# Sample attention of a hybrid decoder step: value gathers asked for after the logits, and all key turns between logits and products

## The chip, the core and the metric

The kernel runs on one core of one Trainium2 chip. The metric is the device time of one launch in microseconds (us). The kernel before takes 1688.96 us, the median of three runs (1687.34 to 1699.0).

## What is computed

The reference is one layer of a decoder, for a prompt group (512 tokens) and a sample group (8 sequences of 8 new tokens, 64 rows in all). What matters here is the attention of the sample group. For each of its 64 rows an indexer has picked 256 keys out of 4096 cached ones; their keys and values are gathered from a paged cache, and every row attends to its own 256 keys (and to new ones where they were picked):

```
def attend_selected(q, kg, vg, valid):
    logits = jnp.einsum('bqhd,bqkhd->bqhk', q, kg).astype(jnp.float32) * (HEAD_DIM ** -0.5)
    logits = jnp.where(valid[:, :, None, :], logits, -jnp.inf)
    p = jax.nn.softmax(logits, axis=-1).astype(vg.dtype)
    return jnp.einsum('bqhk,bqkhd->bqhd', p, vg)
```

There are 8 heads of 64 columns, so a gathered row of keys or of values is 512 float32, 2 KB.

## The kernel before, in words

Every engine runs one long list of jobs, in an order that a planner writes down before the program is built (`JOBS`). TensorE (PE), ScalarE (ACT) and VectorE (DVE) walk lists made from the same plan, so the plan sets what waits behind what on each of them. GpSimd (POOL) has its own list in the code, and issues the gathers.

**The sample attention** works on 16 groups (`NGR`) of 4 rows (`GQ`). For group g:

- `gather_keys(g, j)` (L873, POOL): two indirect DMAs of 128 rows of 2 KB for row j into `kunit`. For g > 0 it first waits until the same place was turned for the group before.
- `T(g, j)` (`turn_keys`, L991, PE; `keys_act`, L1378, ACT): 8 transposes of row j's keys into two PSUM banks, and two copies into `kts`. ACT first waits for the logits of the group before, which read `kts`. PE's next turn waits for the copy before the last.
- `QK(g)` (`logits`, L1002 and L1008, PE): 4 matmuls with the bias (8 records) and 16 with the keys (32 records), each 8 output rows wide in its own quarter of the array. It waits for `OM` of the group before and for the last copy of the keys. At its end it raises `lg_full`.
- `max` (L1848 and L1849, DVE), then `EX` (L1384, ACT): the row maximum and the exponentials. `PT` (L1017 and L1018, PE; L1392, ACT): three transposes of the weights and a copy.
- `gather_values(g)` (L883, POOL): eight indirect DMAs into `vunit`; they wait for `pv_done` of the group before, which read `vunit`.
- `PV(g)` (`values`, L1026 and L1029, PE): the products with the values; it waits for each row's values. Then `om` (L1860, DVE), and `OS(g)` (`own_rows`, L1036, PE).

POOL's order is: the keys of group 0; then for each g the keys of rows 0 to 2 of g + 1, the values of g, and the keys of row 3 of g + 1.

**The plan** around it (`interleaved`): `prompt_jobs` is the prompt's work. It begins with gate projections (`gcP`, `gcS`, L962). Then come its *units*: index scores `pi` (24 jobs, L1087 on PE, L1757 on DVE), 32 attention units `qk`, `pt`, `pv` (L1096, L1103, L1109), with the convolution's norm (`cv`, `croot`, `cn`) and its projection (`cbP`, `cbS`, L1135) between them. Last come the projections `gaP`, `gaS` and `abP`. `sample_jobs` lists the pieces of the sample attention. `cost` gives each job a price on PE in us: a `T` 0.9, `QK` 3.4, `PT` 0.5, `PV` 2.7, `OS` 0.9, `gaP` and `gcP` 6.9, `gaS` and `gcS` 1.8, `abP` and `cbP` 3.5, an index score 0.22 for each 128 keys and so on. `vector_cost` does the same for DVE. The planner puts prompt jobs, and whenever DVE's running total is more than 6 ahead of PE's, it puts pieces of the sample attention until it is not. After the units the pieces left are spread evenly over the jobs left.

In the plan before, QK(0) ends at 24.4 of planned PE time, QK(9) at 164.9; the units end at 249.4 (with group 9's products asked for among them, and no piece in the last 72.8), and the whole list at 411.0.

**DVE's list** (`vector_jobs`) follows the same order, with work of its own in it: 62 taps of the depthwise convolution (L1740 and L1742), all of them ahead of the first index score; and after the scores of each of three prompt tiles 16 rounds of the top-128 selection (L1766 and L1767), of which one is put behind each of DVE's jobs until they run out. The rounds of a tile must be done before that tile's first attention unit.

PE and DVE are tied in both directions: prompt jobs go through a ring of four PSUM banks and, where DVE reads them, a ring of four tiles (`hand_over`, L1346), which ACT fills only when DVE has taken the one of four jobs ago.

## Time and profile before

| | |
|---|---|
| median of 3 runs | 1688.96 us (1687.34 to 1699.0) |
| the profiled execution's own time | 1685.35 us |
| its span, first to last instruction | 1683.5 us |
| PE busy in the span | 1362.8 us (81%) |
| stage of the sample attention, from its first turn of keys to its end | 409.5 to 966.5 us of the span |

Rows of the trace say which engine ran which line, when it began and for how long; in brackets stands how long the engine had been idle before and what ended that ("<-remote": the profile knows the time of the semaphore's update, but no instruction that made it then; "<-issue": nothing that the profile shows). Matmuls are pipelined, and their ends are modelled. "PEclk" is TensorE's granted clock as a share of full speed.

### The profile page before, as it was taken

Reading aid. Unit: us, or ns where it says so; the run is one execution under the profiler, and the core shown is the slowest. Engines: PE = TensorE matmul, PEld = TensorE weight load, DVE = VectorE, ACT = ScalarE, POOL = GpSimd, SP = SyncE. Lnnn points to the kernel's source line nnn. Section 1 sums busy time; section 2 is a strip of 40 time slices with the busy share of each in tenths; the row PEclk is TensorE's granted clock in tenths of the full one; section 3 lists DMA queues with packets and bytes.
Section 4 is the critical chain, followed back from the end, with each engine's and each line's share of the span. In section 5 each row is a group of like instructions: output and inputs, shape, how many; then the busy total and the mean of one; then the engine's idle time right before and its main releaser. Section 6 shows DMA issues by size and latency. Waiting matters only on the chain.

```text
span 1683.5 us, 19141 instructions
## 1 busy us (share of the span) xinstructions
PE 1362.8 (81%) x7392; PEld 791.0 (47%) x7392; DVE 718.3 (43%) x1357; ACT 447.9 (27%) x925; POOL 556.1 (33%) x519
## 2 busy tenths in 40 slices
PE   5799997899578756699999989379987877799860
PEld 5525554565243323355554478267843433344420
DVE  3349999985556555345000211342421111122218
ACT  1531143432224345745333211111110111011110
POOL 1200487864545665400345200000023233234410
PEclk9899998999777877799999979659988989899975
DMA  7602121234545665421355450822069989988613
GB/s 230 209 2 78 51 76 36 67 99 119 149 142 143 178 175 148 120 64 50 115 149 171 127 170 3 313 92 63 7 225 383 350 324 359 355 333 341 252 53 117
DMA packets 91064, 270.85 MB, mean 161 GB/s; under 512 B 17783, under 2 KB 54343, under 8 KB 80407
## 3 DMA queue, kind: packets, MB, share of 16 engines
q1 hardware_dynamic: 52944, 159.35, 25.6%
q0 software_dynamic: 35552, 107.02, 20.7%
q10 hardware_dynamic: 2479, 3.27, 0.6%
q8 instruction: 59, 0.97, 0.2%
q14 instruction: 30, 0.25, 0.0%
HBM read 294.65 MB, written 22.98 MB: 189 GB/s over the span
## 4 chain that ended last, share of the span: by engine, by line
PE 56%; DVE 18%; DMA 9%; ACT 6%; another core or an unknown queue 5%; issue 4%; POOL 1%; SPq 1%; ACTq 0%; POOLq 0%; DVEq 0%
PE ps L962 9%; PE ps L1275 9%; PE ps L968 7%; DMA arena<-in_w_gu,arena 6%; PE ps L1141 4%; PE ps L1135 4%; PE ps L1300 4%; DVE arena L1666 4%; DVE arena L1665 4%; DVE arena L1667 4%; PE ps L991 3%; PE ps L1026 2%; PE ps L1257 1%; PE ps L1158 1%
## 5 line engine op out<-in xcount | busy, mean ns | idle before, releaser
L962 PE MATMUL ps<-arena 128*128 128x64 f32 (+3 forms) x1216 | 344.7, 450 | 9.3 <-ACT arena L1471 8.7
L962 PEld LDWEIGHTS ps<-arena 128*128 128x128 f32 (+1 forms) x1216 | 192.3, 203 | 157.2 <-issue 147.4
L1275 PE MATMUL ps<-arena 128*64 128x256 f32 x1568 | 208.6, 413 | 63.5 <-DMA arena<-in_w_gu,arena 61.7
L873 POOL DMA_INDIRECT arena<-in_cache_k,arena x128 | 126.8, 991 | 251.8 <-PE ps L991 183.4
L1275 PEld LDWEIGHTS ps<-arena 128*64 128x64 f32 x1568 | 115.7, 148 | 153.0 <-DMA arena<-in_w_gu,arena 75.0
L883 POOL DMA_INDIRECT arena<-in_cache_v,arena x128 | 124.2, 970 | 83.9 <-PE ps L1029 49.1
L991 PE MATMUL ps<-arena 128*128 128x128 f32 x512 | 87.9, 318 | 64.2 <-ACT arena L1378 47.9
L968 PE MATMUL ps<-arena 128*128 128x256 f32 (+5 forms) x640 | 134.8, 376 | 3.0 <-ACT arena L1480 2.2
L1346 ACT ACTIVATE arena<-ps 128x256 f32<-128x256 f32 (+5 forms) x148 | 61.2, 418 | 276.2 <-PE ps L1141 65.8
L924 POOL DMA_INDIRECT scr_ypair<-arena x49 | 50.5, 1030 | 242.8 <-ACT arena L1600 238.8
L968 PEld LDWEIGHTS ps<-arena 128*128 128x128 f32 (+1 forms) x640 | 112.3, 202 | 25.4 <-issue 5.2
L991 PEld LDWEIGHTS ps<-arena 128*128 128x128 f32 x512 | 68.0, 164 | 95.3 <-issue 89.0
L849 POOL TENSOR_TENSOR arena<-arena 128x816 f32<-128x816 f32 x58 | 102.9, 1775 | 8.9 <-ACT arena L1364 1.4
L917 POOL DMA_INDIRECT arena<-scr_x,arena x49 | 49.7, 1015 | 164.9 <-DVE arena L2018 148.6
L2039 DVE COPY arena<-ps 128x128 f32<-128x128 f32 x49 | 14.3, 292 | 210.6 <-PE ps L1285 210.6
L1378 ACT ACTIVATE arena<-ps 128x512 f32<-128x512 f32 x128 | 71.6, 595 | 117.8 <-remote 64.9
L1300 PE MATMUL ps<-arena 128*64 128x512 f32 x392 | 94.9, 604 | 0.5 <-issue 0.5
L1135 PE MATMUL ps<-arena 128*128 128x64 f32 (+1 forms) x256 | 81.9, 475 | 5.5 <-ACT arena L1526 3.4
L1594 ACT ACTIVATE arena<-ps 128x128 f32<-128x128 f32 x49 | 13.6, 278 | 258.9 <-PE ps L1275 209.9
L2024 DVE COPY arena<-ps 128x512 f32<-128x512 f32 x49 | 33.9, 692 | 113.7 <-PE ps L1257 88.7
L1665 DVE MAX8 arena<-arena 128x8 f32<-128x2052 f32 x32 | 73.6, 2299 | 1.1
L1666 DVE FIND_INDEX8 arena<-arena 128x8 uint32<-128x2052 f32 x32 | 73.3, 2290 | 0.0
(311 smaller groups left out, 1745.4 us busy)
## 6 DMA issues: line engine op xcount, KB each, us to landing
arena<-in_w_gu SPq DMA_DIRECT2D x32, 2048.0 KB
arena<-in_w_dn SPq DMA_DIRECT2D x32, 1024.0 KB
arena<-in_w_in SPq DMA_DIRECT2D x20, 1024.0 KB
arena<-in_w_attn_out SPq DMA_DIRECT2D x8, 512.0 KB
arena<-in_w_o SPq DMA_DIRECT2D x4, 1024.0 KB
arena<-in_w_pg SPq DMA_DIRECT2D x4, 1024.0 KB
arena<-scr_ypair SPq DMA_DIRECT2D x4, 1024.0 KB, 6.4
arena<-in_x_prompt SPq DMA_DIRECT2D x4, 512.0 KB, 11.9
```

Source lines behind the costliest of these rows:

```text
L849: nc.gpsimd.tensor_tensor(a[:, 0:CLEN], a[:, 0:CLEN], p[:, 0:CLEN], ALU.add).then_inc(conv_add, 1)
L873: pl.indirect_dma_start(kunit[:, 2 * j + t, :], None, I["cache_k"], bass.IndirectOffsetOnAxis(ap=offs[:, t, n:n + 1], axis=0)).then_inc(k_ ...
L883: pl.indirect_dma_start(vunit[:, 2 * j + t, :], None, I["cache_v"], bass.IndirectOffsetOnAxis(ap=offs[:, t, n:n + 1], axis=0)).then_inc(v_ ...
L962: mm = nc.tensor.matmul(out, w[:, k], hT[:, k, a:b], start=(k == 0), stop=(k == KC - 1))
L968: mm = nc.tensor.matmul(out, hT[:, k, at:at + rows], w[:, k], start=(k == 0), stop=(k == KC - 1))
L991: mm = nc.tensor.transpose(PS[4 + m % 2][:, c * P:(c + 1) * P], kunit[:, 2 * j + t, c * P:(c + 1) * P], ident)
L1135: mm = nc.tensor.matmul(ps[:, 0:n], w[:, c], src[:, c, at:at + n], start=(c == 0), stop=(c == CC - 1))
L1275: mm = nc.tensor.matmul(PS[2 + p % 2][64 * half:64 * half + 64, 0:2 * P], xT[:, p % 3, j, 64 * h:64 * h + 64], w[:, k, half, :], start=(k ...
L1300: mm = nc.tensor.matmul(PS[5 + p % 2][64 * half:64 * half + 64, :], hidT[:, p % 2, c * 64:c * 64 + 64], w[:, c, half * 512:(half + 1) * 51 ...
L1378: nc.scalar.activation(kts[:, j, :, t * P:(t + 1) * P], PS[4 + m % 2].rearrange("p (c k) -> p c k", c=CC), cp).then_inc(k_act, 1)
L1665: step(V.max(m, work))
L1666: V.max_index(idxu[:, r * 8:r * 8 + 8], m, work)
```

## The change

It does four things. In the pieces of a group the last turn of the next keys, `T(g+1, 3)`, moves from behind `PV(g)` to in front of it. The planner no longer puts a `PV` until its own count of PE time is more than 14 (`VALUES_LATER`) past the `QK` that it put last; until then it puts prompt jobs, even where DVE is behind. On POOL the values of group g are asked for only when `lg_full` tells that the logits of g are done. And the keys of all four rows of g + 1 are asked for ahead of the values of g.

```diff
@@ sample_jobs
-        jobs += [("QK", g)] + turned[0] + [("EX", g)] + turned[1] + [("PT", g)] + turned[2] + [("PV", g)] + turned[3] + [("OS", g)]
+        jobs += [("QK", g)] + turned[0] + [("EX", g)] + turned[1] + [("PT", g)] + turned[2] + turned[3] + [("PV", g), ("OS", g)]
@@ interleaved
+VALUES_LATER = 14.0
...
-    pe = dve = rounds = 0.0
+    pe = dve = rounds = asked = 0.0
+
+    def ready(piece):
+
+        return piece[0] != "PV" or pe > asked + VALUES_LATER
 
     def put(job):
-        nonlocal pe, dve, rounds
+        nonlocal pe, dve, rounds, asked
         jobs.append(job)
         pe += cost(job)
+        if job[0] == "QK":
+            asked = pe
         dve += vector_cost(job)
...
-        while dve > pe + 6 and pieces:
+        while dve > pe + 6 and pieces and ready(pieces[0]):
             put(pieces.pop(0))
     per, credit = sum(cost(j) for j in rest) / max(1, len(pieces)), 0.0
     for piece in pieces:
-        jobs.append(piece)
+        while rest and not ready(piece):
+            credit -= cost(rest[0])
+            put(rest.pop(0))
+        put(piece)
         credit += per
         while rest and credit > 0:
             credit -= cost(rest[0])
-            jobs.append(rest.pop(0))
+            put(rest.pop(0))
     return jobs + rest
@@ POOL
             def gather_values(g):
+                pl.wait_ge(lg_full, g + 1)
                 if g:
                     pl.wait_ge(pv_done, g)
...
             for g in range(NGR):
                 if g + 1 < NGR:
-                    for j in range(GQ - 1):
+                    for j in range(GQ):
                         gather_keys(g + 1, j)
                 gather_values(g)
-                if g + 1 < NGR:
-                    gather_keys(g + 1, GQ - 1)
```

## Rows read from the trace of the kernel before

**Rows 1.** The page: PE's total, and its granted clock in 40 slices.
```profile
PE 1362.8 (81%) x7392; PEld 791.0 (47%) x7392; DVE 718.3 (43%) x1357; ACT 447.9 (27%) x925; POOL 556.1 (33%) x519
PEclk9899998999777877799999979659988989899975
```

**Rows 2.** Busy time of each engine in four stretches of the stage.
```profile
core 0: us, PE busy (x) PEld busy (x) DVE busy (x) ACT busy (x) POOL busy (x), PEclk, DMA share, GB/s
409.50:516.00 106.50, 73.15 (x428) 40.23 (x428) 59.22 (x139) 33.62 (x62) 56.94 (x55) 0.78 0.50 143
516.00:716.00 200.00, 135.84 (x836) 66.70 (x834) 101.59 (x283) 100.46 (x213) 114.51 (x120) 0.78 0.56 157
716.00:803.50 87.50, 84.07 (x376) 46.36 (x375) 43.61 (x119) 44.22 (x126) 1.89 (x2) 0.99 0.17 54
803.50:966.50 163.00, 158.80 (x893) 78.44 (x891) 19.99 (x46) 52.11 (x92) 68.69 (x72) 1.00 0.48 141
```

**Rows 3.** The pieces of the chain of waits, 515 to 640 us: start, length.
```profile
519.09 11.06 another core or an unknown queue
...
569.39 10.41 another core or an unknown queue
```

**Rows 4.** DVE's row maximum (L1848): what ended the idle time before its 16 instances.
```profile
  remote: 60.9, 10
  PE ps L1008: 59.2, 6
```

**Rows 5.** PE's logits (L1002, L1008) and DVE's row maximum in groups 0, 1, 5, 9 and 10.
```profile
415.60 2.34 PE L1008 MATMUL ps<-arena 128*8 128x320 f32 x32 [0.17 <-ACT arena L1378]
429.34 0.49 DVE L1848 TENSOR_REDUCE arena<-ps 128x1 f32<-128x320 f32 x1 [14.64 <-remote]
...
452.36 2.34 PE L1008 MATMUL ps<-arena 128*8 128x320 f32 x32
456.68 0.49 DVE L1848 TENSOR_REDUCE arena<-ps 128x1 f32<-128x320 f32 x1 [2.12 <-remote]
...
569.81 2.34 PE L1008 MATMUL ps<-arena 128*8 128x320 f32 x32
579.85 0.49 DVE L1848 TENSOR_REDUCE arena<-ps 128x1 f32<-128x320 f32 x1 [6.64 <-remote]
...
683.46 0.49 DVE L1848 TENSOR_REDUCE arena<-ps 128x1 f32<-128x320 f32 x1 [3.21 <-PE ps L1008]
...
811.57 2.34 PE L1008 MATMUL ps<-arena 128*8 128x320 f32 x32
813.97 0.49 DVE L1848 TENSOR_REDUCE arena<-ps 128x1 f32<-128x320 f32 x1 [13.81 <-PE ps L1008]
```

**Rows 6.** POOL's gathers: first values of groups 1, 5 and 15, and the last.
```profile
450.17 0.94 POOL L883 DMA_INDIRECT arena<-in_cache_v,arena  x1 [7.99 <-PE ps L1029]
...
565.41 0.94 POOL L883 DMA_INDIRECT arena<-in_cache_v,arena  x1 [1.23 <-PE ps L1029]
566.66 0.94 POOL L883 DMA_INDIRECT arena<-in_cache_v,arena  x1 [0.30 <-issue]
...
576.84 0.94 POOL L873 DMA_INDIRECT arena<-in_cache_k,arena  x1 [0.30 <-issue]
...
953.95 0.95 POOL L883 DMA_INDIRECT arena<-in_cache_v,arena  x1 [0.30 <-issue]
```

**Rows 7.** PE, next steps behind group 1's logits, and group 15's products.
```profile
458.14 1.09 PE L991 MATMUL ps<-arena 128*128 128x128 f32 x4 [2.42 <-issue]
...
467.86 1.12 PE L991 MATMUL ps<-arena 128*128 128x128 f32 x4 [1.55 <-issue]
...
961.25 1.90 PE L1026 MATMUL ps<-arena 128*8 128x512 f32 x16 [0.74 <-ACT arena L1392]
```

**Rows 8.** DVE's groups of instructions by form, 410 to 966 us.
```profile
L1742 DVE SCALAR_TENSOR_TENSOR arena<-arena 128x512 f32<-128x512 f32 x46 | 34.6, 753 | 1.6
L1766 DVE MAX8 arena<-arena 128x8 f32<-128x384 f32 x16 | 8.9, 557 | 0.3
L1767 DVE MATCH_REPLACE8 arena<-arena 128x384 f32<-128x384 f32 x16 | 8.7, 543 | 0.0
```

## The prediction

> **What bounds the kernel now.** The page first: PE is busy for 1362.8 of 1683.5 us, and its granted clock sags in the second quarter and again later [rows 1]. The stage of the sample attention lies in that second quarter, so the table of stretches comes next. From 409.5 to 716 PE is busy for 73.2 + 135.8 of 306.5 us, and its granted clock is 0.78, a mean of the two levels of 2.4 and 1.2 GHz. From 716 to 966.5 it is busy for 242.9 of 250.5 us at 0.99 to 1.00 [rows 2]. All the idle time worth having, 97.5 us, lies ahead of 716. DVE is busy for 161 us there, ACT 134 us, POOL 171 us: none is full, so it is waiting.
>
> The chain of waits names what is waited for: pieces of 11.06 and 10.41 us, the second of them beginning at 569.39, inside QK(5), that the profile puts down to nobody [rows 3, 5]. DVE's row maximum waited 60.9 us in ten groups for an update of PE's semaphore that came later than the modelled end of the matmuls [rows 4]. The modelled end of QK(0) is 415.60 + 2.34 = 417.9, and the maximum began at 429.3, 11.4 us late; in group 1 it was 2.0 us late, in group 5 7.7, in group 10 0.06 [rows 5]. What differs is POOL. In groups 1 and 5 it had begun the values 2.2 and 4.4 us before, and it issues one gather every 1.25 us, ten in a row up to 577.8 [rows 6]; in group 10 nothing was under way, for POOL was busy for 1.9 us in all from 716 to 803.5 [rows 2]. So logits that run while values are being gathered come late, by up to 11 us, and PE, ACT and DVE all stand. That is the cost the change can reach. How much of it can go is another matter, since the change also writes a new plan.
>
> **The new plan, and its price.** I went through the planner's arithmetic for both orders, job by job, and added up for each interval from one QK to the next PE's planned cost and DVE's work. DVE's prices are from its rows: a tap 0.75 and 0.28, 1.0 with both halves, and a round on 384 keys 0.56 + 0.54 and some 0.17 for its load and gaps, 1.27 [rows 8]; a round on 256 or 512 keys and the short jobs are scaled from these by width.
>
> Before, the nine intervals from QK(0) to QK(9) plan 18.0, 19.8, 20.7, 14.8, 16.4, 12.0, 12.4, 11.9 and 14.5 on PE, and 17.9, 20.1, 22.4, 13.2, 17.9, 14.2, 17.6, 17.8 and 12.6 on DVE. The larger of each pair sums to 157.3. The trace took 683.4 - 417.9 = 265.5 us [rows 5], 108.2 more. Of this 55.8 is late logits (60.9 less some 5 for group 14 [rows 4]); 52.4 is left, 5.8 a group, for the chain maximum, exponentials, turned weights, for turns that run slowly and for the half clock.
>
> After, a group holds 11.0 of its own pieces and at least 10.1 of prompt work between the turns and PV, so the units have ended with QK(8) rather than with group 9. The intervals to QK(1), QK(2) and so on plan 26.7, 21.4, 21.2, 21.4, 21.2, 21.2, 22.1 and 21.3 on PE, and then 30.7 to the end of the units, at 231.6. DVE's are 25.9, 33.0, 39.6, 56.8, 7.1, 10.6, 7.8, 9.3 and 23.2. DVE's work was spread evenly and now piles up in the intervals to QK(2), QK(3) and QK(4), which hold 8, 20 and 20 of the 48 rounds: the planner used to put pieces when DVE was behind, and now it may not. DVE becomes the bound there, 129.4 us against 64.0.
>
> The sum, from 417.9:
> - QK(0). The values no longer run beside it, only the keys of group 1, eight gathers from 410.8, so some 10 us. I let its result come at 422.5, 4.6 us late instead of 11.4; bounds 0 and 11.4.
> - The first four intervals at the larger price: 26.7 + 33.0 + 39.6 + 56.8 = 156.1.
> - The next four on PE, 85.8. The prompt units cost more than planned: 716 to 803.5 is 87.5 us [rows 2] for a planned 72.8, a factor of 1.20. On the prompt part of these, 10.1 to 11.0 each, that is 2.1 each: 94. The rest of the units, 30.7 x 1.20 = 37.
> - Waits of the chain, 4.5 for each of eight intervals, 36. Bounds 2 (nothing but max, exponential and weights behind one another) and 5.8 (as before, slow turns and half clock with it); I go near the upper.
> - So the units end at 422.5 + 156.1 + 94 + 37 + 36 = 745.6; before 803.5.
> - The rest plans 411.0 - 231.6 = 179.4; before, 161.6 planned took 163.0, a factor of 1.01 [rows 2]. 181, to 926.6.
> - The new wait puts the value gathers beside the turns. Behind QK(1) that is how it was already: from 456.7 to 469.0 PE did turns of 24 transposes and the weights, with idle pieces of 2.42 and 1.55 us before turns, put down to nobody [rows 5, 7]. Four records of 1.1 us, one each 2 to 3 us, is 1 to 2 us lost a turn, on turns that are not hidden. I take 2 us a group in the 11 groups where PE is the bound, 22 us; bounds 0 and 5 (55 us).
>
> That ends the stage at 948.6 instead of 966.5, 18 us sooner. Behind the stage nothing of the list changes, and PE starts it later or sooner as a whole. The profiled execution took 1685.35 us, 3.6 below the median of the runs; from it 1667.5, and against the median 1671. I forecast **1670 us**.
>
> **What costs nothing, and why.** The values are asked for 0.3 us after the logits; eight take 10 us, and the last lands at most 6.4 us behind its issue: group 15's products started at 961.25 waiting for ACT, not for values whose last gather had ended at 954.9 [rows 6, 7]. 16.7 at most, against at least 14 planned and some 16 to 20 real: hidden, and up to 2.7 us a group (40 us) if it weren't. Behind the waiting value gathers on POOL stand the keys of the group after next, which must wait for turns that come behind the same QK anyway; they are asked for 10 to 20 us behind it and needed 21 us or more behind it. POOL's 16 gathers make 20 us, under every interval. The key turn moved in front of PV costs PE the same 1 us, and the two gathers moved in front of the values the same 2.5. Wait instructions themselves are nothing at this scale.
>
> A rule of the Trainium skill speaks against the change: "Trainium Architecture — The Big Picture", section "What this means for kernel authors", says that SBUF has separate sides for engines and for DMAs that can't contend. The trace shows logits late whenever values are gathered and not otherwise [rows 5, 6], which doesn't bear the rule out as the whole story, though it doesn't show the place either. What it would make of the time is the last rival.
>
> **The rivals.**
> - *Only the logits were hurt.* The turns run freely, and the chain costs 2 to 3 us a group instead of 4.5, since the clock stays up. That takes 22 + 16 off: 1632 to 1645. For it: the long stall of rows 3 begins inside a QK. Against: the turns of rows 7.
> - *The stall moves into the turns, slower than before.* Behind QK(1) the next steps took 12.2 us with values on the way; where PE is the bound this costs 5 us, not 2, in all 11 groups: 33 more, and DVE, bound in three intervals, stands during those turns too, 3 x 3. 1670 + 42 = 1712, slower by 1.4%. It decides from a loss of 3.7 us a group: there the gain of 18 is gone. In the last seven groups there was no stall to win, so there each microsecond is a loss.
> - *Keys take the values' place.* Values and keys now make one run of 20 us behind each QK. Where an interval is shorter than 23 us, the next QK falls into its end. The planned 21.2 are below that, the real ones I expect at 26; in the last seven groups four are 21.6. 4 x 4 us: 1686.
> - *Gathers are innocent.* The late logits stay with the new, longer plan, 6.1 us each (60.9 over ten [rows 4]) for the eight of the units, 49, and 7 for QK(0): 56 on the forecast, 1726. Against: group 10 [rows 5].
>
> **How the numbers follow.** The forecast, 1655 to 1684, has 0.42; only the logits 0.24; moved into the turns 0.16; keys 0.12; gathers innocent 0.06. The largest doubt in the sum is the DVE-bound stretch, 129.4 us worked out from prices, plus or minus 10. The range goes from 1626, the first rival and something of this, to 1708. A measurement tells some 1% from no change, 1672 and 1706. Faster: all of the first rival, 0.24, somewhat over half of the forecast, 0.23, and 0.05 of keys, 0.52. Slower: 0.13 of the second and the fourth's 0.06, 0.19. Within 1%: 0.29.
>
> **What would show it.** The row maximum's idle put down to nobody falls from 60.9 to under 15 us. In the stretch to QK(4), about 603, DVE is busy over 75% and PE under 60%. The units end near 746 (803.5), the stage near 949. The granted clock behind QK(4) is over 0.9. Turns behind each QK show idle pieces of 1 to 3 us put down to nobody. Wrong it is if the logits stay late with no value gather on the way, if PV waits for values, or if the stretch to QK(4) takes much over 190 us.

## The result, and the profile after

The kernel after takes **1791.26 us**, the median of four runs (1786.48 to 1793.88), against 1690.53 for the kernel before in its four: a ratio of 1.059, 95% interval 1.056 to 1.062. It is 5.9% slower. The forecast was 1670, and the range ended at 1708; both were missed.

PE's totals on the page of the kernel after, and its granted clock in 40 slices:

```profile
PE 1392.5 (78%) x7392; PEld 804.3 (45%) x7392; DVE 720.5 (40%) x1357; ACT 455.2 (25%) x929; POOL 557.4 (31%) x519
PEclk9899998998766588889887897956998898999985
```

PE is busy for 29.7 us more than in [rows 1], with the same number of instructions: the same work, most of it at a lower granted clock. The span is 104.7 us longer, so nearly three quarters of the loss is idle time.

DVE's row maximum (now L1859), what ended the idle time before it, kernel after:

```profile
  PE ps L1019: 60.6, 15
  remote: 7.9, 1
```

This answers to [rows 4], and it is what was forecast. The late logits have gone, from 60.9 us in ten groups to 7.9 in one. The time didn't follow, and one reason is that the row maximum is only one taker of PE's results. The same kind of wait, for an update of PE that comes later than the profile models it, now stands in front of ACT. Two later traces of the unedited kernels, both from the third set below, 405 to 1080 us; the three longest such waits of each (us in total, times, longest), before and after:

```profile
DVE arena L1848 <- remote: 68.6, 10, 17.0
ACT arena L1378 <- remote: 61.8, 7, 18.3
ACT arena L1346 <- remote: 31.3, 3, 11.2
```

```profile
ACT arena L1357 <- remote: 39.1, 10, 8.9
ACT arena L1389 <- remote: 16.6, 8, 7.1
ACT arena L1524 <- remote: 16.5, 4, 4.9
```

L1378 and L1389 are the copies of turned keys. L1346 and L1357 are one line, `hand_over`, and L1524 takes a unit's product: these are results of the prompt's jobs. So the late results have not gone: this waiting has moved from the logits and the keys to the prompt's jobs for the most part. (An idle time that ends so is not all lateness; it says which results came late, not by how much.)

The table of stretches of the kernel after: the first four of [rows 2], and what has come behind them (columns as there), for the stage's last `own_rows` now ends at 1074.0 instead of 968.8.

```profile
409.50:516.00 106.50, 75.67 (x414) 39.78 (x413) 68.61 (x165) 37.14 (x69) 58.88 (x56) 0.80 0.52 149
516.00:716.00 200.00, 112.99 (x585) 54.94 (x586) 96.42 (x270) 89.38 (x204) 46.70 (x49) 0.68 0.24 67
716.00:803.50 87.50, 69.66 (x351) 33.14 (x350) 22.86 (x60) 25.65 (x66) 37.91 (x39) 0.86 0.48 142
803.50:966.50 163.00, 136.33 (x737) 75.21 (x738) 21.36 (x57) 55.90 (x106) 59.33 (x63) 0.90 0.41 118
966.50:1077.00 110.50, 88.31 (x445) 41.99 (x444) 17.66 (x33) 29.38 (x52) 40.09 (x42) 0.87 0.43 128
```

From 516 to 716 PE now does 585 matmuls where it did 836, and no engine is busy for more than 57% of the time. POOL issued 49 gathers instead of 120: far fewer groups went through. From 803.5 to 966.5 PE was full before (158.8 us); now 26.7 of 163 us are missing.

The same table cut at the row maxima of groups 0 to 4, 5, 8, 9 and 15:

```profile
420.80:452.50 31.70, 29.05 (x143) 14.66 (x144) 24.39 (x54) 9.58 (x16) 18.21 (x16) 0.86 0.48 135
452.50:492.80 40.30, 26.75 (x155) 14.73 (x154) 33.22 (x80) 15.12 (x30) 17.77 (x16) 0.75 0.42 123
492.80:551.30 58.50, 30.39 (x138) 12.81 (x137) 35.81 (x99) 21.91 (x43) 15.53 (x16) 0.65 0.25 72
551.30:633.30 82.00, 39.75 (x184) 20.95 (x183) 51.55 (x143) 52.48 (x113) 15.11 (x16) 0.58 0.18 52
633.30:671.00 37.70, 26.38 (x142) 12.30 (x142) 6.55 (x20) 9.60 (x24) 15.51 (x16) 0.82 0.40 112
671.00:786.00 115.00, 82.38 (x461) 40.22 (x460) 24.34 (x72) 33.59 (x87) 45.48 (x48) 0.82 0.46 133
786.00:856.00 70.00, 62.97 (x330) 34.12 (x331) 22.93 (x58) 32.64 (x73) 16.07 (x16) 1.00 0.27 75
856.00:1056.00 200.00, 163.35 (x863) 85.97 (x861) 19.89 (x46) 56.69 (x96) 84.01 (x88) 0.85 0.46 134
```

The fourth line is the worst: 82 us, in which PE, DVE and ACT are busy for 40, 52 and 52, at a granted clock of 0.58, so nearly all at the lower of the two levels (1.2 GHz). One group, nine attention units (five on 128 keys, four on 256) and four norms run in it. Nothing is full, so the engines wait for one another. PE's waits in that stretch say for whom:

```profile
PE ps L1114 <- DVE arena L1794: 18.6, 7, 6.1
PE ps L1107 <- issue: 6.8, 1, 6.8
PE ps L1134 <- DVE arena L1842: 5.2, 3, 3.0
```

L1114 is a unit's transpose, which needs DVE to have weighed the exponentials that ACT has made; L1134 is the norm's, with DVE in front of it too. Of ACT's 52 us here, 21.8 are 17 table loads (`ACT_TABLE_LOAD`, 1.28 us each), at the lines of the units' exponentials (8), of the norms (8) and of the group's exponentials (1).

And in the gate stage, PE's timeline behind group 9 in the kernel after:

```profile
866.54 0.60 PE L1002 MATMUL ps<-arena 128*128 128x128 f32 x4
872.53 1.11 PE L1002 MATMUL ps<-arena 128*128 128x128 f32 x4 [5.39 <-issue]
```

This is a turn of keys, and in the middle of it PE stands for 5.39 us. The last of eight value gathers was issued at 864.92, 2.2 us before PE stopped, and four key gathers follow it up to 869.93. The same piece is 4.56 us at 941.27 and 3.76 at 1007.68. In the gate stage, part of the stall that was in QK (10 and 11 us, [rows 3]) is now in the turns.

### The profile page after: what moved, and what is told of

The parts are those of the page before. It is cut to its first block, busy times and chain, and to the rows that moved or that the text cites. A ratio compares the mean times of both kernels' runs of the same rounds, so it can differ in the third digit from the quotient of the medians.

```text
span 1788.2 us, 19169 instructions
## 1 busy us (share of the span) xinstructions
PE 1392.5 (78%) x7392; PEld 804.3 (45%) x7392; DVE 720.5 (40%) x1357; ACT 455.2 (25%) x929; POOL 557.4 (31%) x519
## 4 chain that ended last, share of the span: by engine, by line
PE 53%; DVE 21%; issue 9%; DMA 8%; ACT 5%; another core or an unknown queue 2%; POOL 1%; SPq 1%; POOLq 0%; ACTq 0%; DVEq 0%
PE ps L1286 9%; PE ps L973 8%; PE ps L979 6%; DMA arena<-in_w_gu,arena 5%; PE ps L1146 5%; PE ps L1311 4%; PE ps L1152 4%; DVE arena L1677 4%; DVE arena L1676 4%; DVE arena L1678 4%; PE ps L1002 3%; PE ps L1019 2%; PE ps L1268 1%; PE ps L1169 1%
## 5 line engine op out<-in xcount | busy, mean ns | idle before, releaser
L973 PE MATMUL ps<-arena 128*128 128x64 f32 (+3 forms) x1216 | 349.8, 455 | 9.3 <-ACT arena L1482 8.7
L973 PEld LDWEIGHTS ps<-arena 128*128 128x128 f32 (+1 forms) x1216 | 197.6, 209 | 155.4 <-issue 145.7
L1357 ACT ACTIVATE arena<-ps 128x256 f32<-128x256 f32 (+5 forms) x148 | 60.9, 418 | 286.7 <-PE ps L1146 73.9
L979 PEld LDWEIGHTS ps<-arena 128*128 128x128 f32 (+1 forms) x640 | 111.9, 201 | 25.1 <-issue 5.2
L1146 PE MATMUL ps<-arena 128*128 128x64 f32 (+1 forms) x256 | 94.0, 530 | 21.7 <-ACT arena L1357 10.7
L1002 PE MATMUL ps<-arena 128*128 128x128 f32 x512 | 84.2, 313 | 34.2 <-issue 26.7
L1389 ACT ACTIVATE arena<-ps 128x512 f32<-128x512 f32 x128 | 71.8, 596 | 136.2 <-PE ps L1002 112.5
L1002 PEld LDWEIGHTS ps<-arena 128*128 128x128 f32 x512 | 65.8, 161 | 56.5 <-issue 54.6
L1146 PEld LDWEIGHTS ps<-arena 128*128 128x128 f32 x256 | 49.9, 247 | 57.0 <-issue 49.7
```

The costliest lines, as they stand in the source:

```text
L973: mm = nc.tensor.matmul(out, w[:, k], hT[:, k, a:b], start=(k == 0), stop=(k == KC - 1))
L979: mm = nc.tensor.matmul(out, hT[:, k, at:at + rows], w[:, k], start=(k == 0), stop=(k == KC - 1))
L1002: mm = nc.tensor.transpose(PS[4 + m % 2][:, c * P:(c + 1) * P], kunit[:, 2 * j + t, c * P:(c + 1) * P], ident)
L1146: mm = nc.tensor.matmul(ps[:, 0:n], w[:, c], src[:, c, at:at + n], start=(c == 0), stop=(c == CC - 1))
L1389: nc.scalar.activation(kts[:, j, :, t * P:(t + 1) * P], PS[4 + m % 2].rearrange("p (c k) -> p c k", c=CC), cp).then_inc(k_act, 1)
```

## The experiments

Three chips were used (which of them, if any, the comparison above ran on is not on record), and the kernel before isn't equally fast on them: it took 1611.2 us on the chip of the first set (one run), 1690.3 on the second and 1681 to 1690 on the third. Each run is compared within its chip. For the reading of all sets, the starts of DVE's row maximum in six groups, each from the trace of one execution (us; the first four kernels on the first chip, the others on the third):

| kernel | g0 | g3 | g4 | g9 | g10 | g15 | time |
|---|---|---|---|---|---|---|---|
| plan alone | 420.4 | 552.3 | 624.8 | 841.1 | 864.4 | 1002.9 | 1731.1 |
| no threshold | 417.2 | 498.1 | 520.8 | 638.6 | 765.5 | 908.7 | 1647.2 |
| POOL's order alone | 418.0 | 494.7 | 518.5 | 640.2 | 769.2 | 911.4 | 1644.4 |
| turn alone | 418.5 | 496.4 | 518.9 | 636.8 | 763.5 | 906.6 | 1634.6 |
| before | 431.6 | 533.4 | 558.2 | 687.4 | 817.7 | 965.2 | 1688.9 |
| after | 419.7 | 551.8 | 632.3 | 854.3 | 887.5 | 1057.1 | 1795.0 |
| before, no values | 431.3 | 505.2 | 521.2 | 616.5 | 745.6 | 885.4 | 1607.3 |
| after, no values | 422.7 | 545.1 | 617.4 | 799.0 | 822.2 | 961.3 | 1692.3 |
| before, limit at group 6 | 429.9 | 524.7 | 549.6 | 832.6 | 861.9 | 990.7 | 1714.3 |
| after, limit at group 6 | 422.2 | 552.7 | 633.2 | 879.5 | 912.5 | 1071.2 | 1808.9 |
| POOL's order alone | 419.8 | 497.6 | 528.5 | 667.2 | 797.3 | 954.4 | 1695.9 |
| threshold off beside narrow units | 423.1 | 538.6 | 569.1 | 728.4 | 857.8 | 1037.8 | 1770.8 |

### One part at a time

**The plan alone**: the new plan with POOL's order of before.

```diff
-                pl.wait_ge(lg_full, g + 1)
...
-                    for j in range(GQ):
+                    for j in range(GQ - 1):
                         gather_keys(g + 1, j)
                 gather_values(g)
+                if g + 1 < NGR:
+                    gather_keys(g + 1, GQ - 1)
```

> The new plan with GpSimd's old order of gathers (values asked for when the products of the group before are done, the last keys behind them, no wait for the logits). Theory P, the plan is what costs: it makes VectorE the bound up to QK(4) and puts a group's turns, exponentials and weights side by side; then nearly all of the 101 us is here, 1760 to 1800 us, and the stretch to QK(4) still ends near 633. Theory V, the value gathers beside the turns are what costs: then most of it is gone, 1700 to 1730, though the logits are late again by some 6 us each.

**POOL's order alone**: the same diff the other way round, on the plan of before.

> The plan of before with GpSimd's new order (all keys of g+1, then the values of g behind the wait for its logits). Theory P: near before, 1675 to 1705, the logits no longer late. Theory V: the stall moves into the turns and into PV, which in this plan comes 5 to 10 us behind QK, so that values asked for at QK also arrive late for it: 1730 to 1800.

**No threshold**: the whole change but this.

```diff
-VALUES_LATER = 14.0
+VALUES_LATER = 0.0
```

> Everything of the change but VALUES_LATER = 0: the next keys' last turn is in front of PV and the values wait for the logits, but the planner may put PV at once. Theory P: 1680 to 1710. Theory V: as the run with the gather order alone, 1730 to 1800, for PV comes before its values. The difference to the changed kernel is what the threshold alone costs or gives.

**The turn alone**: the kernel before with the last turn in front of PV.

```diff
-        jobs += [("QK", g)] + turned[0] + [("EX", g)] + turned[1] + [("PT", g)] + turned[2] + [("PV", g)] + turned[3] + [("OS", g)]
+        jobs += [("QK", g)] + turned[0] + [("EX", g)] + turned[1] + [("PT", g)] + turned[2] + turned[3] + [("PV", g), ("OS", g)]
```

> Only the last turn of the next keys moved in front of PV; planner and GpSimd as before. Both theories: 1685 to 1700. If it is above 1710, the moved turn is a cost of its own, because it makes GpSimd's last keys of g+1 (behind the values of g) be needed earlier.

They took 1731.1, 1644.4, 1647.2 and 1634.6, one run each, beside a kernel before of 1611.2. The expectations were made on a kernel before of 1690, so only differences can be compared. The plan with its threshold costs 120 us here (theory P had 70 to 110), while the whole rest of the change costs 36. The table says where: the plan alone is at 624.8 in group 4, where the kernel without the threshold is at 520.8. POOL's order alone costs 33, between the two theories (up to 15, or 40 and more), and the turn alone 23, more than the 20 above which it was to count as a cost of its own.

No trace of the kernel before was taken on this chip. But the four traces show a wait that it doesn't have in its traces on the others: PE for a gather that hasn't landed, 405 to 1090 us (total, times, longest), for the plan alone, POOL's order alone, no threshold and the turn alone:

```profile
PE ps L1003 <- DMA arena<-in_cache_k,arena: 36.3, 9, 6.5
PE ps L1025 <- DMA arena<-in_cache_v,arena: 23.5, 20, 1.9
PE ps L1037 <- DMA arena<-in_cache_v,arena: 21.0, 16, 2.8
PE ps L991 <- DMA arena<-in_cache_k,arena: 20.6, 6, 4.8
```

With the turn moved in front of PV and POOL's old order, the keys of the last row are asked for behind the values and come too late for it. With the new order and no threshold, the values are asked for too late for PV. These waits are of the size of the three smaller steps. They also say that the 120 us of the plan alone aren't all the plan's: up to 36 are late keys, a mismatch that the whole change doesn't have (there PE waits for gathers 2.3 us in all).

What had not been expected: no logits are late in any of them. The row maximum of the plan alone, with the old order of gathers:

```profile
  PE ps L1020: 61.9, 16
```

All 16 instances wait for PE as the profile models it, and none for an update without a maker; nor does any other engine in this trace. So the stall on which the forecast rested isn't there on this chip, and its kernel before is 79 us faster. Did the values still cause it on the other chips? That had to be asked by itself, below.

### DVE's pile-up, first look

The second set repeats both kernels and runs both with 4 of the 16 selection rounds of each prompt tile, so 36 of the 48 rounds are left out.

```diff
-                step(V.max(mv8, sc))
-                step(V.match_replace(sc, mv8, sc, TAKEN))
+                if r < 4:
+                    step(V.max(mv8, sc))
+                    step(V.match_replace(sc, mv8, sc, TAKEN))
```

> The kernel before, unedited, for its trace: 1611 us and no late result where the chip is as in the four runs above; the stage of the sample attention then ends near 890 instead of 966.

> The changed kernel, unedited, beside the kernel before in the same rounds. If the late results of TensorE are a property of the chip that the first runs fell on (in the four runs above no result was late and before took 1611 us), then on this chip too the logits are in time, before is near 1611, and the change costs what the plan alone did: 1731 or a little less with the gathers behind the logits, 1720 to 1745, so 110 to 130 us. If the late results belong to the kernels, before is near 1690 and this 1790.

> The kernel before with the same rounds left out. Theory D: before is bound by VectorE nowhere for long, so it falls by at most 20 us, and the difference between the two kernels shrinks by 20 or more. Theory L: both fall alike.

> The changed kernel with 4 instead of 16 rounds of the selection for each prompt tile (12 of 48 are computed; the rest is left out). 36 rounds are some 45 us of VectorE. Theory D (VectorE piled up on the way to QK(4) is the bound): this falls by 38 to 48 us against the changed kernel. Theory L (each group's chain of logits, exponentials, weights and turns stands alone now, with no prompt work in it, and PE idles there): it falls by under 20.

The kernels again: 1691.2 and 1791.3 (four runs), beside 1690.3, a ratio of 1.060 (1.056 to 1.063); this chip shows late logits, so the guess of 1611 was wrong. With few rounds, before 1688.6, after 1768.6, one run each. The rounds are hidden before (some 2 us) and not after (some 23, between the two theories), so some 20 of the 100 us are DVE's, and 80 aren't.

### Nearly all of DVE's work away

The taps go as well: of each tap but the first, 8 of 512 prompt columns are computed. This and the rounds are left out of the computation of both kernels.

```diff
-                out = (convo[:, c, 0:NP], convo[:, c, NP:N].rearrange("p (b q) -> p b q", b=NB))
-                src = (gluP[:, c, w:w + NP], gluS[:, c, :, w:w + NQ])
+                n = NP if w == 0 else 8
+                out = (convo[:, c, 0:n], convo[:, c, NP:N].rearrange("p (b q) -> p b q", b=NB))
+                src = (gluP[:, c, w:w + n], gluS[:, c, :, w:w + NQ])
```

> The kernel before once more, for its trace on the chip of this set; nothing is changed. The single edits lay at 1634 to 1647 us beside a kernel before of 1611 on a chip where no result of PE came late, and the last row maximum of that kernel isn't known. If this chip is of that kind I expect some 1611 us, no piece put down to nobody in the row maximum's idle, the intervals between row maxima in the units at 21 to 27 us as in the single edits, and the last row maximum at 880 to 890, which would put their 25 us inside the stage. If it is of the other kind, 1690 us and 55 to 65 us of late logits again.

> The change whole and once more. Where results come late (a kernel before of 1690) it is 1791 again. Where they don't (1611), the theory that the new plan alone costs gives what the plan alone cost there, 1731, and at most 25 us more from the gathers' order: 1731 to 1756, a ratio of 1.075 to 1.09. The theory that value gathers beside turns cost by themselves on any chip would give more than 1765.

> The kernel before with VectorE's own work nearly gone: 12 of the 48 selection rounds are kept, and of each depthwise tap but the first only 8 of the 512 prompt columns are computed (so 36 rounds and most of the taps are left out of the computation). That takes some 45 us of rounds and some 40 us of taps off DVE. In the plan before they lie beside other work, so I expect little, 5 to 25 us less than the kernel before on the same chip.

> The change with the same work left out (36 of 48 rounds, and 504 of 512 prompt columns of each tap but the first). If the pile-up on DVE is what makes the new plan slow, its intervals up to QK(4) fall to PE's planned 21 to 27 us plus the chain, and the stage loses nearly all of its 100 us: this kernel within 20 us of the other one with the work left out. If the cause is that prompt work stands alone between turns and products, each job handed from PE to ACT or DVE and back with nothing beside it, then DVE's work hardly matters: 30 to 40 us go at most, and it stays 60 us or more above the other.

Before 1688.9 (one run; 1690.2 in seven beside the others) and after 1795.0 (four runs; 1.060, 1.055 to 1.065). Light, before 1677.3 and after 1771.2: 94 us apart, where the whole kernels are 105. The second theory had this, 60 or more. The stretch from group 3 to group 4 of the light kernel after:

```profile
554.20:627.30 73.10, 38.77 (x183) 20.87 (x184) 28.82 (x91) 52.30 (x113) 15.15 (x16) 0.60 0.20 58
```

DVE is down from 52 to 29 us, and the stretch is down from 80.5 to 73 us only, at a clock of 0.60. A full DVE isn't what bounds it. My forecast had priced exactly this interval by DVE's load.

### Values and plan apart

Two pairs in the fourth set, on the same chip as the third. In the first, values are gathered for group 0 alone, and PE takes those in every group, so the value gathers of 15 groups are left out (in the kernel after, POOL still waits for each group's logits before it asks for the next keys). In the second, no sample piece from QK(6) on may lie among the units.

```diff
             def gather_values(g):
                 if g:
-                    pl.wait_ge(pv_done, g)
+                    return
```

```diff
-        while dve > pe + 6 and pieces:
+        while dve > pe + 6 and pieces and pieces[0] != ("QK", 6):
```

> The kernel before with the values gathered for group 0 alone; PE multiplies those of group 0 in every group (the value gathers of 15 groups are left out, so their 120 issues on POOL and their transfers). If the value gathers are what makes PE's results late, none is late here even on a chip that shows them (the row maximum's idle put down to nobody 0 instead of 61 us) and the time falls from 1690 to 1611 to 1630. If the key gathers do it as well, a good part of the 61 us stays.

> The change with the values of 15 groups left out in the same way. The plan with its threshold stays. If the plan itself costs, it stays 90 to 120 us above the other kernel without values, so 1710 to 1750. If the value gathers beside turns are the main cost, it comes within 40 us of it.

Before 1607.3, after 1692.3: 85 us apart. Two things follow. The values cost the kernel before 79 us (against the 1686.0 of the same set) and the kernel after 103 (against its 1795.0 in the third set), so moving them didn't win the 79 back, it added some 20. And with no values on the way the plan costs 85 us. Both came out a little below what was expected, 1611 to 1630 for the one, and 1710 to 1750 and 90 to 120 above it for the other.

What the values cost the kernel after, and where, is read from the same jobs with and without them: from group 4 to group 8, four groups with the same 602 matmuls, first with values, then without, and PE's projections (L1146) in each.

```profile
632.30:784.40 152.10, 109.51 (x602) 53.01 (x603) 30.80 (x91) 43.14 (x111) 61.03 (x64) 0.82 0.43 128
L1146 PE MATMUL ps<-arena 128*128 128x512 f32 (+1 forms) x96 | 39.1, 562 | 18.3 <-ACT arena L1357 12.1 <-issue 6.2
```

```profile
617.40:729.80 112.40, 98.26 (x602) 48.23 (x602) 30.53 (x92) 42.88 (x111) 30.68 (x32) 0.97 0.34 99
L1146 PE MATMUL ps<-arena 128*128 128x512 f32 (+1 forms) x96 | 31.9, 478 | 2.9 <-ACT arena L1357 2.9
```

The value gathers make 39.7 us of these 152.1, ten a group. PE is idle for 28 us more, 15.4 of it in front of the projections, and 11 us slower at its work, at a granted clock of 0.82 instead of 0.97. The turns are the same in both (280 ns a record, 2.4 us of waiting). So here the gathers hit the prompt's jobs that the threshold has put behind the turns.

Where the plan's own share lies is seen best in this pair, as little comes late in it (ACT's copies of prompt jobs waited 7.3 us for late results, with keys alone on the way). Without values, the kernel before from group 5 to group 9, and the kernel after from group 3 to group 4:

```profile
540.30:616.50 76.20, 59.07 (x457) 29.67 (x458) 56.88 (x157) 53.08 (x114) 30.68 (x32) 0.90 0.39 111
```

```profile
545.10:617.40 72.30, 39.35 (x183) 20.51 (x183) 51.44 (x143) 52.47 (x113) 7.57 (x8) 0.60 0.11 30
```

The times are nearly the same, and so are the busy times of ACT (53.08 and 52.47 us) and DVE. In the first, PE has done four groups (128 records of L1008), in the second one (32 of L1019). The prompt's part is not the same, though: PE began eight units in the first, one of them on 256 keys, and nine in the second, four of them on 256, and finished more there; copies of turned keys make 17.2 us of ACT's time in the first and 4.5 in the second. By the planner's prices the first holds 50.8 us of PE's work and the second 21.2. So the pair shows that four groups and fewer units fit into the time of one group and more units. How many groups the units' chain hid, it doesn't show. After, the threshold lets nothing of the sample group in there, and those groups come later, up to group 8 in intervals of 26 to 31 us in which PE is busy for 87% (98 of 112.4 us).

The row maxima of the pair, set against the plan, say how much is lost where. Up to group 4 the kernel after is 96 us later than the other and 17 further on in the plan: 79 lost. Of that, 29 are lost by group 3 already, before the long row of units: PE waits 7.8 us for DVE in front of one `own_rows` (L1047), with taps and index scores ahead of it on DVE. Up to group 10, 22 are won back. Up to group 15 another 19 go, and the rest of the 85 behind it.

> The kernel before, but the planner stops putting sample pieces among the units when the next would be QK(6): ten groups instead of six lie among the gate projections, with 9.8 of planned projections to a group instead of 16. QK(5) to QK(9) took 104 us for 49 planned; these pieces plan 44 and would go at 1.01 there, and POOL's 20 us of gathers a group still fit under 21. If pieces among units are what is dear, and pieces among projections run at their plan, it ends 30 to 55 us sooner than the kernel before. If a group's chain needs the wider cover, or POOL becomes the bound, it is level or up to 20 us slower.

> The change with the same limit: groups 6 to 15, each still with 14 of planned work between QK and PV, which is now filled from the gate projections and not from the units. In the change QK(5) stood at 670, and from there to the end of the stage at 1077 it took 408 us for 256 planned. Theory of the units alone between turns and products: the rest of the units takes 53 us by themselves (44 planned at 1.2), and the 212 left go at 1.0 to 1.1, so the stage ends at 935 to 960 and the kernel takes 1650 to 1675. Theory of the value gathers beside the turns: the 212 go at 1.4, as the last groups of the change did (33 to 38 us for 21 to 27), and the kernel takes 1735 or more. Between 1675 and 1735 both have a part.

1714.3 (1.017, 1.008 to 1.026) and 1808.9 (1.073, 1.064 to 1.082). The first is 28 us slower, where at most 20 was expected. The second lies in the branch of the value gathers (1735 or more), and groups 6 to 15 take 1.49 times their plan; but group 5 to group 6 took 105.6 us for 73.2 planned, so the price of the units was too low in it as well. The kernel before with the limit, three stretches of the table:

```profile
600.00:716.00 116.00, 86.77 (x323) 46.52 (x324) 69.09 (x194) 69.84 (x176) 0.00 (x0) 0.76 0.08 23
716.00:803.00 87.00, 76.67 (x454) 40.34 (x452) 18.46 (x50) 35.77 (x72) 30.26 (x32) 0.97 0.41 121
803.00:966.00 163.00, 141.12 (x823) 70.48 (x822) 15.63 (x40) 53.11 (x92) 91.55 (x96) 0.92 0.57 168
```

From 600 to 716 the units run without a single gather, and PE is busy for 87 of 116 us at a clock of 0.76. So units by themselves don't run at 1.2 times their plan. That factor came from the wide ones behind 716 [rows 2]; all 32 here plan 84 us and, with one group of 11, took 169.5. Behind it, ten groups share the projections that six had, 9.8 us each instead of 16, and PE, idle for 5.6 us of these 163 in the kernel before, now is for 22. Spreading the sample group thinner over the projections is no way out.

### The last two

The gathers' order alone once more, now where results come late, and the whole change with the threshold lifted beside the norm and the first units:

```diff
-        while dve > pe + 6 and pieces and ready(pieces[0]):
+        while dve > pe + 6 and pieces and (ready(pieces[0]) or job[0] in ("cv", "croot", "cn")
+                                          or job[0] in ("qk", "pt", "pv") and job[1] < 12):
```

> The old plan with the new order of POOL alone, which cost 33 us where no result came late. If this chip shows late results (a kernel before near 1690): were the late logits the loss that the gathers' order could win back, it would gain 40 to 60 us of them and stand at 1650 or less. If the values only take their cost along into the turns, as the difference of the kernels without values says, the row maximum's idle put down to nobody falls under 15 us and the time is still not lower: 1695 to 1725.

> The whole change, but the planner may put a PV before its 14 us are over while the prompt's jobs are the convolution's norm or attention units of the first tiles (up to unit 11). The threshold stays in the first three groups and from then on, and groups 3 to 8 lie beside the norm and the narrow units again, as before. If the narrow units kept alone are the cost of the plan, the row maxima from group 3 to group 8 come 22 to 27 us apart, group 10 comes 55 to 75 us sooner than in the change (888), and the kernel takes 1715 to 1740. If the threshold costs the same wherever it is held, the three groups that keep it give a quarter of the cost and the new order of the gathers the rest: also near 1735, but if the loss sat in how values and turns meet, groups 3 to 8 would still be 33 us or more apart and the time over 1750.

**The order alone** takes 1695.9 beside 1681.1: 1.010 (1.007 to 1.014), slower by 1%. The second theory held in both numbers; the late logits went from 68.6 us to this:

```profile
  PE ps L1007: 60.1, 10
  remote: 7.7, 1
```

And for a while it does win: group 9 comes 20 us sooner than in the kernel before. It has given 10 of that back by group 15, and then the rest. PE behind the last logits, with the order alone and in the kernel before:

```profile
L1025 PE MATMUL ps<-arena 128*8 128x512 f32 x16 | 7.4, 927 | 5.2 <-DMA arena<-in_cache_v,arena 4.1 <-ACT arena L1391 1.1
```

```profile
L1026 PE MATMUL ps<-arena 128*8 128x512 f32 x16 | 1.9, 593 | 0.7 <-ACT arena L1392 0.7
```

The last group's values, asked for behind its logits, aren't there in time: 4.1 us of waiting, and products that take 7.4 us instead of 1.9. Both kernels begin the output projection at 994 to 995. The two traces are of executions of 1689.5 and 1688.9 us, the second from an earlier set, so they show where the win goes, but not where the 1% lies.

**The threshold lifted** gives 1770.8, 1.055 (1.051 to 1.058). I had expected 1715 to 1740. Group 10 comes 30 us sooner than in the change, not 55 to 75, since groups 3 to 8 are 29 to 31 us apart, on 11 to 12 us of plan, and not 22 to 27. The chain of waits in one such interval:

```profile
626.67 3.62 PE ps L1020 x32
630.28 0.50 issue
630.78 0.94 POOL arena L897
...
641.17 0.30 issue
641.47 3.53 DMA arena<-in_cache_v,arena
645.00 0.04 issue
645.05 2.56 PE ps L1038 x10
```

Logits, then eight value gathers and their landing, 14.7 us from 630.3 to 645.0, then the products: with next to nothing of the prompt in between, the new wait puts the gathers on the path of such a group. That is half of the interval. Another part is late results once more: the products before these end at 616.87 as modelled, and DVE's `om` and an ACT copy take results of PE only at 622.71, while key gathers follow the values up to 619.8. And from group 10 on, where its plan is that of the kernel before but for the order inside a group, the next three come 38 to 39 us apart instead of 30. PE's turns there, over four groups, in this kernel and in the kernel before:

```profile
L1003 PE MATMUL ps<-arena 128*128 128x128 f32 x129 | 21.8, 307 | 20.6 <-ACT arena L1390 19.0 <-issue 1.6
L1038 PE MATMUL ps<-arena 128*8 128x512 f32 x64 | 12.8, 944 | 0.0
```

```profile
L991 PE MATMUL ps<-arena 128*128 128x128 f32 x136 | 19.9, 279 | 4.6 <-issue 3.0 <-ACT arena L1392 1.6
L1026 PE MATMUL ps<-arena 128*8 128x512 f32 x64 | 7.6, 593 | 0.0
```

Turns wait for 20.6 us instead of 4.6, and the products behind them take 944 ns each instead of 593. So of the 7.7 us a group (150.4 us over four against 119.5), 4 are the stall and 1.3 the products. Of the rest, 1.6 us a group are the projections, at 461 ns a record instead of 423 (240 records). The whole change shows the same turns over its four groups, and the one without values doesn't:

```profile
L1002 PE MATMUL ps<-arena 128*128 128x128 f32 x128 | 24.3, 342 | 21.7 <-issue 16.1 <-ACT arena L1389 5.6
```

```profile
L1002 PE MATMUL ps<-arena 128*128 128x128 f32 x160 | 24.5, 298 | 2.3 <-ACT arena L1389 1.4 <-ACT arena L1403 0.7
```

No version was found that is faster than the kernel before.

## Why the prediction was wrong

**Right.** QK(0) was forecast at 422.5, and its maximum began at 420.8, 4.6 us late as forecast. The late logits fell under 15 us. They come from value gathers on the way: without values, the kernel before waits 17.8 us there in one group, group 0, whose values it still gathers, instead of 68.6 in ten. DVE's work did pile up behind QK(1), and PE was busy for 59% up to QK(4). The rest of the units behind QK(8) was given 37 us and took 39.7 (786.1 to 825.8).

Two things were asked of the sum: a price of the plan, and a price of the values beside it. The kernel after without values separates them, stretch by stretch, in us (the first comparison's kernel after, and the third chip's without values; the forecast with its chain waits):

| from the row maximum (or end) | forecast, without the 22 for values | without values | with values |
|---|---|---|---|
| QK(0) to QK(4) | 174.1 | 194.8 | 212.5 |
| QK(4) to QK(8) | 112 | 112.4 | 152.8 |
| QK(8) to the end of the units | 37 | 39.1 | 39.7 |
| the rest of the stage | 181 | 205.9 | 248.2 |

**Wrong, and the larger part: "I take 2 us a group in the 11 groups where PE is the bound, 22 us".** With the same plan, the values make 101 us (the last two columns), and 103 between the kernels' times. The bound was 55. The first four intervals had been given nothing for it, and took 18; the next four had 8, and took 40; the last seven had 14, and took 42. The forecast looked for the stall in the turns alone. In the last seven groups it is largely there: in four of them (the L1002 row of the whole change, in the last experiment) turns waited for 5.4 us a group, and their records were slower, 342 ns against 298. Between QK(4) and QK(8) it isn't: there it stands in front of the projections and units, which the threshold had put where the values are on the way. The granted clock there was 0.82, and not over 0.9 as forecast; without values it was 0.97. The rival "the stall moves into the turns" had the mechanism and its point of decision at 3.7 us a group; it had 16% and 1712 us, and its 5 us a group were too little too.

**Wrong: the larger of two sums as the length of an interval.** "The first four intervals at the larger price" and their four chain waits made 174.1 us. Without values they took 194.8, so this step was 21 us short; with them 212.5, well over the 190 that was set as a sign of being wrong, with DVE busy for 145.0 of it, 68% and not over 75%. A unit goes PE, ACT, DVE, ACT, DVE, PE, ACT, PE, and the ring lets a few into it at a time; from QK(3) to QK(4), with DVE busy for 52 us or for 29, it took 80.5 and 73 us (third chip), so no engine's load says its time. The factor of 1.20 that I used for prompt work came from the one stretch where units are widest. For the next four intervals and the end of the units the sum without values was right to 3 us.

**Wrong: the factor of 1.01 for the rest.** Without values the rest of the stage took 205.9 us where 181 was forecast, 25 short. The five groups from group 10 took 139.1 for a planned 120.0 with the new plan (1.16), 139.8 for 139.2 with the old. Why the same kinds of jobs go slower in the new order isn't shown.

**The balance.** What was to be won was real: the kernel before is 79 us faster without values. But in their new place the values cost 103, and the plan costs 85 without them.

**Wrong: "16.7 at most ... hidden".** Value gathers behind the logits are hidden only where a fill lies in between. The whole change has one, and waits for values 2.3 us in all. In the last group, 7 us planned are left, and the order alone lost some 10 us there; where the threshold was lifted, 14.7 us lay on the path of a group.

**The missed reading.** The intervals of the kernel before held a hint. From QK(5) to QK(9) they plan 12 to 14 on PE and took 20 to 31. I put all of that to late logits and a chain wait of 5.8 us a group. Without values they still take 14 to 25: part of the difference was ACT and DVE at work on rounds and units, and not waste.

**The other rivals.** "Gathers are innocent" falls: without values the late logits go and 79 us with them. "Only the logits were hurt" falls by the turns. The rule cited from the Trainium skill, "Trainium Architecture — The Big Picture", section "What this means for kernel authors", that engines and DMAs use separate sides of SBUF and can't contend, had been put to this use: if nothing contends, the gathers are innocent and the time is 1726. That use fails on the third chip, where 79 us hang on whether the values are on the way. The rule itself is neither borne out nor refuted, since no run shows at which place the updates are held up, in SBUF or elsewhere. On the first chip nothing comes late.

**What stays open.** Why the first chip shows no late results, and what the values would cost there. Where the updates are held up. Why the rest of the stage runs at 1.15 times its plan even without values. What makes the intervals up to QK(3) longer: without values 122.5 us for 69.3 planned, against 73.9 for 58.5, and with DVE's work nearly gone they are no shorter (132.9 us with values, where the whole kernel has 132.1). A lower threshold wasn't tried.

## What to carry to other kernels

Before moving work out from between jobs that go back and forth between engines, ask what it was hiding: add up not only each engine's load in the interval but the length of one job's chain through all engines, and take the longest (a rule drawn from one miss, no run here tests it as a forecast). A price for filler work must come from the filler that will stand there, not from the best stretch of its kind. And a stall that goes with a transfer moves with the transfer, onto whatever runs there: before moving the transfer, take it out in one run, to see what the stall costs at all and whether this chip has it. A sign that watches one taker of the late results, as the row maximum here, only says that this one is free of them.

## What the hardware showed that had not been expected

The same kernel took 1611 us on one chip (one run) and 1681 to 1691 on two others. Some 79 us are the price of the value gathers on the third: taken out, it gives 1607. On the first chip, in the traces of four edited kernels with the gathers in place, no engine found a result of PE late. And the stretch from QK(3) to QK(4), with PE busy for 48 to 54% of it in three kernels, ran at a granted clock of 0.58 to 0.60, so what little PE did was slow as well: the products of the units (L1120) took 431 ns a record there without values, and 283 from QK(4) to QK(8) of the same kernel, at 0.97.
